# Gate sums as a second stream of TensorE products under attention, norms and recurrence, and a merge split in two stages

## The reference

```
px_a, px_b, px_c, px_d, px_g = split(hx @ w_in[l])           # px_g: 1024 gate columns
silu_gates = split(silu(px_g), 4)
for i in range(4):
    term = sigmoid(h @ w_gate[l, i]) * ((branches[i] * silu_gates[i]) @ w_branch[l, i])
    acc = term if acc is None else acc + term
return acc @ w_out[l]
```

## Time and profile before

| what | value |
|---|---|
| median of 3 runs | 4609.15 us |
| profiled execution, its own time | 4606.4 us |
| its span | 4604.6 us |
| mean granted TensorE clock | 0.893 of full speed |
| HBM read, written | 183.65 MB, 28.57 MB |

### The profile page before, as it was taken

How to read it: one execution, slowest core, us unless ns; L and a number is a source line. 1 busy time by engine, 2 the same in 40 slices (tenths; PEclk the granted TensorE clock), 3 DMA queues, 4 the chain that set the end, 5 groups by cost and what they waited for, 6 DMA issues and landing times. The chain is left out here.

```text
span 4604.6 us, 66084 instructions
## 1 busy us (share of the span) xinstructions
PE 3641.5 (79%) x25892; PEld 2836.6 (62%) x25892; DVE 2131.8 (46%) x3505; ACT 1222.2 (27%) x2024; POOL 639.7 (14%) x1054
## 2 busy tenths in 40 slices
PE   5877985775688699999875777977674886899987
PEld 2753664653577578888662653655562775788875
DVE  4233527945566422222353334528826665222235
ACT  2102314722233221111101202316522332311120
POOL 0000005500444100000000000005302442000000
PEclk7877997987899899999997878988886999999998
DMA  4000000010211111111334000010001110211132
GB/s 157 32 30 18 6 32 6 0 39 1 54 37 36 50 64 40 51 51 42 113 96 161 36 28 17 7 35 0 11 26 29 46 36 28 81 55 60 55 111 91
DMA packets 95739, 214.86 MB, mean 47 GB/s; under 512 B 9408, under 2 KB 45248, under 8 KB 94400
## 3 DMA queue, kind: packets, MB, share of 16 engines
q1 hardware_dynamic: 95552, 212.26, 13.8%
HBM read 183.65 MB, written 28.57 MB: 46 GB/s over the span
## 5 line engine op out<-in xcount | busy, mean ns | idle before, releaser
L89 PE MATMUL ps<-hh,wh_mg 128*128 128x512 f32 (+1 forms) x1280 | 473.2, 370 | 20.9 <-DVE wl_mg L1982 20.9
L90 PE MATMUL ps<-hl,wh_mg 128*128 128x512 f32 (+1 forms) x1280 | 472.9, 369 | 0.0
L91 PE MATMUL ps<-hh,wl_mg 128*128 128x512 f32 (+1 forms) x1280 | 472.5, 369 | 0.0
L1999 DVE TENSOR_TENSOR dv<-sg_mg,ps 128x256 f32<-128x256 f32 (+1 forms) x160 | 101.5, 634 | 692.8 <-PE ps L91 606.9
L89 PEld LDWEIGHTS ps<-hh,wh_mg 128*128 128x128 f32 x1280 | 243.0, 190 | 62.0 <-issue 21.7
L1948 ACT ACTIVATE sg_mg<-ps 128x256 f32<-128x256 f32 (+1 forms) x160 | 89.0, 556 | 716.8 <-PE ps L91 716.7
L90 PEld LDWEIGHTS ps<-hl,wh_mg 128*128 128x128 f32 x1280 | 243.0, 190 | 40.1
L91 PEld LDWEIGHTS ps<-hh,wl_mg 128*128 128x128 f32 x1280 | 242.8, 190 | 40.3
L1713 DVE TENSOR_TENSOR T_dr<-T_dr,ps 64x256 f32<-64x256 f32 x400 | 167.6, 419 | 158.3 <-PE ps L1490 148.7
L505 POOL TENSOR_TENSOR sq_na<-raw_la 128x512 f32<-128x512 f32 (+1 forms) x18 | 15.7, 897 | 1508.1 <-SPq L75 1502.0
L788 PE MATMUL ps<-kk_da,qs_da 128*128 128x512 f32 (+1 forms) x400 | 134.0, 446 | 102.1 <-ACT qk_da L932 71.1
(11 more groups left out here) (335 smaller groups left out, 8406.6 us busy)
## 6 DMA issues: line engine op xcount, KB each, us to landing
w_mg<-in_d_wmerge SPq DMA_DIRECT2D x64, 640.0 KB, 3.8
w_mod<-in_d_wmod SPq DMA_DIRECT2D x12, 2048.0 KB, 19.4
R_dr<-decay_rows SPq DMA_DIRECT2D x80, 256.0 KB, 4.5
acc_ou<-merged SPq DMA_DIRECT2D x18, 512.0 KB, 5.3
w_gb<-in_d_win SPq DMA_DIRECT2D x16, 512.0 KB, 4.4
w_ou<-in_d_wout SPq DMA_DIRECT2D x8, 1024.0 KB, 8.9
w_gm<-in_d_winr SPq DMA_DIRECT2D x8, 784.0 KB, 7.2
w_pn<-in_d_win SPq DMA_DIRECT2D x12, 512.0 KB, 3.4
```

The costliest lines, as they stand in the source:

```text
L89: pe.matmul(out, w_hi, x_hi, start=first, stop=False)
L90: pe.matmul(out, w_hi, x_lo, start=False, stop=False)
L91: return pe.matmul(out, w_lo, x_hi, start=False, stop=last)
L1999: dve.tensor_tensor(dst, sg[:, u % 2, 0:width], m.ps[:, 4 + u % 4, 0:width], ALU.mult).then_inc(multiplied, 1)
```

## The change

A class `Dense` issues the gate sums in pieces within other phases. A unit is one column tile of weights, loaded in two halves of 256 KB through one buffer `raw`: 8 units from `w_in`, then 32 from `w_gate`. Its work is counted in split products of three matmuls; 8 of them finish a chunk of a unit. Layer 0 has 40 x 24 = 960 of them, layer 1 has 40 x 16 = 640. Four engines take part:

```diff
+    def load(self, sp, point=None, most=None):
+        ...
+            if self.loaded:
+                sp.wait_ge(self.low, self.loaded)
+            src = m.d_win[self.l, T_GATE + u][:, k:k + 4] if u < 8 else m.d_wmerge[self.l, u - 8][:, k:k + 4]
+            sp.dma_start(self.raw[:], src).then_inc(self.w_in, 16)
+    def tensor(self, pe, point=None):
+        while self.q < self.upto(point):
+            ...
+            if k == 0 and chunk >= self.start // KD + len(self.banks):
+                pe.wait_ge(self.moved, chunk - len(self.banks) + 1)
+            if c == 0 and k % 4 == 0:
+                pe.wait_ge(self.low, 2 * u + k // 4 + 1)
+            mm = split_products(pe, m.ps[:, self.bank(chunk), 0:width], ...)
+    def move(self, act, point=None):
+        while (self.chunk + 1) * KD <= self.upto(point):
+            act.wait_ge(self.made, chunk + 1)
+            if chunk:
+                act.wait_ge(self.stored, 16 * chunk)
+            act.activation(self.out[:, 0:width], m.ps[:, self.bank(chunk), 0:width], ACT.Copy).then_inc(self.moved, 1)
+            act.wait_ge(self.moved, chunk + 1)
+            act.dma_start(m.d_raw[:, u, at:at + width], self.out[:, 0:width]).then_inc(self.stored, 16)
+    def cut(self, pool, point=None):
+        while self.half < self.ready(point):
+            pool.wait_ge(self.w_in, 16 * (self.half + 1))
+            if u >= self.AHEAD:
+                pool.wait_ge(self.made, (u - self.AHEAD + 1) * n)
+            pool.tensor_copy(self.wh[:, s], self.raw[:]).then_inc(self.high, 1)
+            pool.wait_ge(self.high, self.half + 1)
+            pool.tensor_tensor(self.wl[:, s], self.raw[:], self.wh[:, s].bitcast(F32), ALU.subtract).then_inc(self.low, 1)
```

```diff
+                            for at, width in far:
+                                mm = score(i, h, a, at, width)
...
+                            fill.tensor(pe, n + 1)
+                            if split and n >= 1:
+                                pe.wait_ge(exp_done, n)
+                            score(i, h, a, *near).then_inc(scored, 1)
```

DVE takes the maximum in two parts. The loops over tiles are written out. The queries of the differential case come by four DMAs per head from a DRAM copy `d_qk`, with one copy and two subtractions by POOL per head. `stack_keys` is replaced:

```diff
+            sp.dma_start(m.d_qk, qk[:]).then_inc(out, 16)
+            ...
+            sp.wait_ge(out, 16)
+            for b in range(2):
+                for a in range(4):
+                    sp.dma_start(raw[b][ROPE * a:ROPE * a + ROPE], m.d_qk[:, 2 + b].rearrange("(j r) c -> r j c", r=ROPE)
+                                 ).then_inc(k_in[b], 16)
+        ...
+            for j in range(MAPS):
+                if j % 4 == 0:
+                    act.wait_ge(k_in[j // 4], 64)
+                act.activation(kk[:, j], raw[j // 4][:, j % 4], ACT.Copy).then_inc(k_high, 1)
+                fill.move(act, j)
```

In `delta_rule` scores move to banks 2 and 3, which the transposes also use; so `grams` follows `update(s, 2)`, `queries` follows `update(s, 4)`, DVE's `scores` comes before its `joined(s, 3)`, and PE waits for them before transposing:

```diff
+                        if b == 3 and s + 1 < STEPS:
+                            for e in range(2):
+                                pe.wait_ge(sem["s_ready"][e], s + 2)
...
+                    rows(s)
+                    fill.cut(pool, POINTS * s)
                     if s + 1 < STEPS:
                         weigh(s + 1)
                         masks(s + 1)
-                        outer(s + 1)
```

`gate_branches` becomes `apply_gates`: it issues the rest of the stream, and for 24 (16) pieces of a chunk it loads a stored gate sum and a branch output through two slots, and ACT and DVE form `yh` and `yl` (`fill.move(act, n)` behind each piece). The last stage of `merge` has the branch products alone:

```diff
+                for u, (f, b, n) in enumerate(products):
+                    if u >= LOGITS:
+                        sp.wait_ge(multiplied, u - LOGITS + 1)
+                    sp.dma_start(logit[:, u % LOGITS, 0:width], m.d_raw[:, 8 + 4 * f + b, at:at + width]
+                                 ).then_inc(logit_in[u % LOGITS], 16)
...
+                    for k in range(2):
+                        mm = split_products(pe, m.ps[:, u % 8, 0:width], wh[:, f % 2, b, k], ...)
+                    mm.then_inc(branched, 1)
...
+                    dve.tensor_tensor(dst, logit[:, u % LOGITS, 0:width], m.ps[:, u % 8, 0:width], ALU.mult
+                                      ).then_inc(multiplied, 1)
...
+                    own = acc[:, f % 2, at:at + width]
+                    pool.tensor_tensor(own, own, term[at_term % TERMS][:, 0:width], ALU.add).then_inc(added, 1)
```

More of the change, by code:

```diff
@@ L480, in _, with normalise_columns @@
                     copy_turned(dve, n, t)
-def normalise_columns(nc, m, l, name, out, tiles, ones, factor, mean, gain, chunks=CHUNKS):
+def normalise_columns(nc, m, l, name, out, tiles, ones, factor, mean, gain, chunks=CHUNKS, rate=4):
     with ExitStack() as st:
@@ L797, in body @@
[L797 to L807 removed]
+                            n = (i * HEADS + h) * maps + a
@@ L1825, in stages @@
-            def stages(eng, cut, move):
-                def body(i, last):
-                    for s in range(2):
-                        for c, (at, width) in enumerate(chunks):
-                            if c == 1 and not (last and s == 1):
-                                cut(i + s, 1 - s)
-                            move(i, s, s * n + c, at, width)
-                cut(0, 0)
-                with eng.Fori(0, tiles // 2 - 1) as i:
-                    body(i, False)
-                body(tiles // 2 - 1, True)
+                sp.wait_ge(fill.stored, 16 * 8 * len(fill.chunks))
@@ L1854, in _ @@
-                stages(act, cut, move)
+                for n, (j, at, width) in enumerate(pieces):
+                    act.wait_ge(into[n % 2], 32 * (n // 2 + 1))
+                    act.activation(gate[:, n % 2, 0:width], gate[:, n % 2, 0:width], ACT.Silu).then_inc(silu, 1)
+                    act.wait_ge(gated, n + 1)
+                    act.activation(yh[:, j, at:at + width], y[:, n % 2, 0:width], ACT.Copy).then_inc(y_high, 1)
+                    fill.move(act, n)
+                fill.move(act)
```

998 lines of the change are left out of this document (563 added, 435 removed).

## The result

The changed kernel takes 4622.81 us (median; 4612.59 to 4626.14, 6 runs) beside 4606.23 us of the kernel before (4602.42 to 4613.31): ratio 1.003, 95% interval [1.0019, 1.004]. It is slower by a third of a per cent; 4330 us had been forecast. The profiled executions have spans of 4610.7 and 4604.6 us.

A forecast was written before the change was run, and what follows sets the result against it. PE was taken to bound the kernel, its 960 us without matmuls lying in crumbs: 4606.4 - 775 (merge) + 13 (`apply_gates`) + 486 (stream elsewhere) = 4330 us; own range 4220 to 4450, 8-in-10 range 4090 to 4610.

The forecast's parts named there:

- The last stage of merge: Merge's last stage, bound by PE: 129 and 111 us instead of 566 and 449, a gain of 775 us.
- apply_gates: Gate stage, 123 and 101 us before: +57 in layer 0, -44 in layer 1, together +13 us.
- the recurrence: Recurrence steps: split products exceed idle PE, new waits, POOL's cuts delay `scores`; +5.8 / +8.0 x 10 = +58 / +80 us.
- The gating MLP: Gating MLP: first weights come 6 us into the phase and the stream starts cold; +10 / +7 us.
- Differential attention: Heads of 7.5 / 7.7 us from stream, shared bank and copies; with context rows and clock, +62 / +57 us.
- stack_maps: Key maps go out and back through memory; 20 us before, PE ends near 46 to 49: +26 / +29 us.
- Short phases bound by DVE: Stream beside DVE's work: `normalise_columns` +2 / +5, latents' norms +5 / +8, both `normalise_turned` +18 / +12, `convolve` +6 / +10 us.
- Latent attention with the rotations: Latent attention, split products and waits for ACT's copy exceeding idle PE: +33 / +38 us; rotations +16 / +21.
- Warmer clock: Phases without any stream, such as `expand_latents` and the next projection, find a warmer clock: -12 / -12 us.
- Nothing is hidden: Rival, all phases outside `apply_gates`: split products delay in full; 843 us instead of 486, total 4712 us, chance 0.13.
- The supply of weights: Rival, dense stream phases of layer 1: loading and cutting weights is the limit; +136 us, total 4466 us, chance 0.12.
- The rule of the Trainium skill: POOL's cuts collide with DVE instructions having two SBUF inputs: at most 180 us, left out of the sum.

The follow-up runs named there:

- x10: Changed kernel with, in the recurrence, POOL's cut of the stream's weights ahead of `rows` and SyncE's stream loads ahead of its `grown` DMAs: 4566.67 us, 0.9914.
- x1: Changed kernel with all 40 units of the stream per layer run in `apply_gates`, none in other phases: 4827.96 us, ratio 1.0482 to the kernel before.
- x3: x2 with three PSUM banks for each map and no wait for the previous exponential before the last 256 scores: 4587.84 us, 0.9962.
- x5: x3 with two raw buffers of queries instead of one and two cut ones instead of three: 4555.24 us, 0.9892.
- x9: x5 with the last 256-column scores of a map issued right behind its first two pieces, as before the change: 4505.1 us, 0.9779.
- x2: Changed kernel with no stream products in the two attentions, these moved to `apply_gates`: 4628.01 us, 1.0047.
- x11: Changed kernel issuing only the first and last split product of each sum of eight; loads, cuts, waits, copies and stores stay: 4368.6 us, 0.948.
- x4: Changed kernel with the stream's loads and cuts six points (three heads) later in differential attention: 4594.95 us, 0.9972.
- x6: Changed kernel with two raw buffers of queries and two cut ones, stream and shared bank kept: 4596.56 us, 0.9975.
- x7: Changed kernel in which POOL cuts only two columns of each tile of a half after the first four halves: 4475.47 us, 0.9709.
- x8: Changed kernel with the stream's products over 64 columns, except the first of each sum of eight: 4605.45 us, 0.9995.

## Why the prediction was wrong

**Right.** The last stage of merge (129 / 111 forecast, 139.9 / 111.4), `apply_gates` (+57 / -44, +55 / -48), and the recurrence in size (+58 / +80, +66 / +89; steps of some 42 us in layer 0, 40 to 43 forecast) and in cause: POOL's cut before `weigh` was given as some 7 us at one go, and x10 takes 20 / 31 us back by moving it with its loads. The gating MLP came out 9 us cheaper. These terms leave 13 us of the 281 by which the span missed the sum (293 by the median). Three small slips of the working move the sum by at most 2 us: 13.6 split products are 7.8 us and not 7.7, the 40 of `convolve` 23.0 us in layer 0 and not 24.7, and the earlier trace rows shows 32 matmuls in 1.10 us and not 16 (a step has 320 of them, so the 5 us stand).

**The step that failed** is "Differential attention: ... I take 7.5 / 7.7: +1.9 / +2.1 x 32", with its premise that only the stream, its bank and its copies change this stage. Measured were heads of 8.8 / 8.5 us and, with `stack_maps`, 143 us more than forecast, half of the miss. Per tile the forecast was +7.6 us for stream and bank together; measured were +13: 7.6 for the stream, 2.5 for the bank and 3.3 for the late scores. In its place the runs show, for layer 0 where nothing else is said:
- the keys' trip through memory, +22 us in `stack_maps` with no stream at all (x1). The trip itself was in the estimate: I had reckoned 46 to 49 us for that stage with the stream, and it took 53 (804.65 to 857.68 in the queue of SyncE). In layer 1 it took 68.5 instead of 49. There the first load of queries stands in SyncE's list behind six loads of the stream:
```profile
3216.55 50.42 SPq L150 DMA_DIRECT2D raw_ds<-in_d_wmerge  x6
3271.54 1.74 SPq L890 DMA_DIRECT2D q_raw_da<-turned_qk  x4
```
  Without the stream (x1) this stage takes 44 us in both layers; that the order of these loads is the cause was not tested.
- queries loaded through one buffer: 26 us in layer 0, 6 in layer 1 (x3 to x5), in the context tiles and the first main one. I had +12 for context rows. That the staging had become four DMAs and three POOL instructions in turn stands in the diff; I priced the stream's instructions and not these.
- the last 256 scores behind values and turns: 3.3 us per tile (x5 to x9). I did name the chain "exponential of one unit, then the last scores, maximum, next exponential", but for the bank's wait alone. The turns in front wait for DVE, and that wait is now inside each head's chain. The higher clock that came with the repair is in the 3.3 us too. This is the largest part that needs no stream.
- the shared bank: 2.5 us per tile (x2 to x3).
- the stream itself: 27.8 to 35.4 us per tile, 7.6 us for 16 split products of 9.2 us. With a quarter of its products, at a clock of 0.80, the tile is still 34.7 us (x11), and at one and the same clock 52 split products cost more than their own time (x11 against x1), so this is not time of PE alone but waits. The one bank and POOL's two duties are the candidates; which of them costs how much was not taken apart: x4 and x6, which each ease POOL alone, took 16 and 11 us off the whole span (some 27 each by the medians).

So a window in which DVE was at 94% and PE at 79% was taken for one with room on PE. The room lay between waits in a fixed order, and the change also lengthened the chain that makes the order.

**Short phases bound by DVE: 68 us more than forecast** (norms of the latents 24, the two turned ones 12, the stage with `convolve` 32). The claim was that DVE's reciprocals cover the stream. The timeline of the changed kernel in `normalise_columns` of the latents:
```profile
329.48 0.89 POOL L195 CAST wh_ds<-raw_ds 128x512 fp32r<-128x512 f32 x1 [2.63 <-DMA raw_ds<-in_d_win]
...
331.73 4.03 POOL L636 TENSOR_TENSOR sq_na<-work_la 128x512 f32<-128x512 f32 x4
333.82 2.87 PE L649 MATMUL ps<-sq_na,const 128*128 128x512 f32 x4 [4.14 <-POOL sq_na L636]
...
336.73 0.69 ACT L662 ACTIVATE std_na<-ps,eps 128x512 f32<-128x512 f32 x1 [9.13 <-PE ps L649]
...
337.45 3.35 DVE L672 RECIPROCAL inv_na<-std_na 128x512 f32<-128x512 f32 x1 [6.80 <-ACT std_na L662]
```
DVE, which bounds the phase, waits 6.80 us: for ACT, for PE, for POOL's squares, which stand behind a cut that waits for its load. Over this stage of layer 0 DVE waits 20.8 us for ACT at this line, 5.9 before the change and 5.5 in x1. The cover is gone at its source. With cheap cuts the longest of these waits is still 6.7 us: POOL then waits 3.36 us for the load alone. x7 (cuts cheap, -8 / -8) and x11 (products fewer, -12 / -6) take shares of the same +19 / +18.

**Latent attention with the rotations: +72 / +75 for +49 / +59.** A quarter of the products brings 41 and 36 us back (x11), and without any the latent stage is at 230 / 211 (x1), 58 / 51 us less than with 55 / 54 us of products: PE's time, not hidden. PE is busy 136.48 of 152 us, 90% (92% before); a pause of 0.43 us per head held nothing of a split product of 0.57.

**"Warmer clock", -24 us,** is not seen: `expand_latents` and the projection of the differential case changed by +0.4 and +1.0 us in layer 0, -0.6 and -1.1 in layer 1, and the mean granted clock went from 0.893 to 0.898 where I had written above 0.95.

**The rivals.** "Nothing is hidden" was given 4712 us at 0.13 and is nearest in size, but wrong in kind: of 843 us some 275 are hidden. It comes near because the forecast had no term of its own for the rebuilt phases, some 195 us without a single product (x1), and neither had any rival. 764 us of gain stand against 568 for the stream in the phases, 195 for the room made for it and 7 in `apply_gates`. The supply of weights, a rival at 0.12 worth +136 us, is met in size by x7 (136), but by chance: x7 removes POOL's cuts everywhere and leaves the loads, and 44 of its 136 us lie in the recurrence, where the forecast had priced the cuts itself.

The rule of the Trainium skill that I left out of the sum (GPSIMD Engine Reference, Key points: GpSimd and VectorE share SBUF interfaces) has no test of its own, but a bound: with cheap cuts DVE's busy time falls from 2015.9 to 1991.2 us (x7), so of the 136 us at most some 25 can be DVE instructions made longer by a cut (what the sharing costs POOL's own instructions is not in this bound). And x10, which leaves the cuts whole and changes only the order, gets back as much in the recurrence as x7 does by making them cheap (20 / 31 against 19 / 25), which speaks for order on POOL.

## What to carry to other kernels

Price the rebuilding apart from the filling: run the kernel with room for the stream and an empty stream (x1) before tuning what fills it. An engine's idle time is room only if the inserted work is behind nothing that the bounding chain needs next; ask for each engine of the stream (PE's products, POOL's cuts, SyncE's loads) which instruction of the chain is queued behind them, and put them where that engine is shown waiting longest. When an operand is split in two so that one piece comes late, look at what stands in the queue between the pieces.

## What the runs showed of the hardware

- Matmuls of these split products over 64 columns follow each other after 0.11 us at full clock, over 256 after 0.12 and over 512 after 0.23 (1040.34, 1040.57, 1040.80 in the changed kernel). Below 256 columns almost nothing is saved here. Whether the product or the load of its weights sets that floor was not told apart.
- Halving the rows that a small matmul reads saved nothing: the inversion's matmuls of 64 columns take 222 ns in the median with 128 rows (L1490 before) and 218 ns with 64 (L1725 after), and 32 in a row 1.15 us in both. That two halves might run side by side, which the forecast left open, is not seen.
- The granted clock of the whole program was lower where PE had less to do: 0.898 with the stream, 0.829 with a quarter of it (PE busy 70%), 0.801 with narrow products (78%). In x8 `stack_maps` with differential attention grew from 412.8 to 438.8 us, at 0.66 instead of 0.86. A test by removal of PE's work is not clean unless the granted clock stands beside it.
- The same matmuls in a tighter chain had a higher clock: 0.86 in tiles of 25 us (x5), 0.96 in tiles of 21.7 us (x9).
